# A two-layer decoder step in exact-split fp32: operand sums for the seven-product tiles moved to GpSimd, and the token mixes spread over the stage ahead and the first pair

## What is computed

```python
def swiglu(h, wg, wu, wd):
    return (jax.nn.silu(h @ wg) * (h @ wu)) @ wd
# D_MODEL = 1024, D_FF = 2816, all float32
x = x + 0.5 * swiglu(rmsnorm(x, norm), w_gate, w_up, w_down)
```

## Time and profile before

| | us |
|---|---|
| three runs: lowest, median, highest | 2516.43, 2526.86, 2526.91 |
| profiled execution, device time | 2519.78 |
| its span, first to last instruction | 2518.0 |
| around the span | 1.8 |

### The profile page before, as it was taken

One profiled execution on the slowest core, in us unless ns is written; L12 is line 12 of the kernel. 1 busy time (PEld: TensorE's weight loads), 2 busy tenths in 40 slices (PEclk: granted clock), 3 DMA queues, 4 the chain that ended last, 5 costly groups with the idle time before them and its releaser, 6 DMA issues. The chain is left out here.

```text
span 2518.0 us, 49302 instructions
## 1 busy us (share of the span) xinstructions
PE 2403.3 (95%) x18705; PEld 2335.5 (93%) x18705; DVE 1521.7 (60%) x2517; ACT 993.8 (39%) x1958; POOL 4.6 (0%) x18
## 2 busy tenths in 40 slices
PE   5999999998999999987999999999999999999998
PEld 5999999865999999977999999999999998999998
DVE  6864864555455555536863865873775656773772
ACT  5432433464455555524432434432433223432431
POOL 0000000000000000000000000000000000000000
PEclk8999999999999999989999999999999999999999
DMA  3323334310211111202333323233233332233232
GB/s 103 100 84 92 100 90 121 94 38 22 60 35 46 48 42 43 59 17 59 88 88 109 92 83 93 76 97 104 84 92 102 93 93 76 85 89 104 84 93 84
DMA packets 373200, 198.91 MB, mean 79 GB/s; under 512 B 31680, under 2 KB 369686, under 8 KB 373064
## 3 DMA queue, kind: packets, MB, share of 16 engines
q1 hardware_dynamic: 372884, 197.03, 27.3%
q10 hardware_dynamic: 180, 0.11, 0.0%
HBM read 194.27 MB, written 2.87 MB: 78 GB/s over the span
## 5 line engine op out<-in xcount | busy, mean ns | idle before, releaser
L408 PE MATMUL ps<-h_hi,w_hi 128*128 128x260 f32 x2112 | 435.9, 288 | 50.2 <-DVE w_lo L536 23.2
L397 DVE TENSOR_TENSOR w_lo<-raw,w_hi 128x512 fp32r<-128x512 f32 (+2 forms) x200 | 200.5, 1002 | 425.0 <-ACT w_hi L391 424.5
L410 PE MATMUL ps<-h_lo,w_hi 128*128 128x260 f32 x2112 | 431.4, 286 | 0.0
L412 PE MATMUL ps<-h_hi,w_lo 128*128 128x260 f32 x2112 | 431.0, 286 | 0.0
L408 PEld LDWEIGHTS ps<-h_hi,w_hi 128*128 128x128 f32 x2112 | 332.8, 193 | 53.7 <-DVE w_lo L536 24.1
L391 ACT CAST w_hi<-raw 128x512 fp32r<-128x512 f32 (+2 forms) x200 | 173.9, 869 | 510.8 <-PE ps L412 480.2
L412 PEld LDWEIGHTS ps<-h_hi,w_lo 128*128 128x128 f32 x2112 | 332.3, 192 | 0.0
L410 PEld LDWEIGHTS ps<-h_lo,w_hi 128*128 128x128 f32 x2112 | 332.1, 192 | 0.0
L408 PE MATMUL ps<-g_hi,w_hi 128*128 128x260 f32 x1408 | 285.1, 284 | 14.0 <-DVE w_lo L397 14.0
L531 ACT CAST w_hi<-raw 128x512 fp32r<-128x512 f32 x280 | 173.3, 622 | 286.5 <-PE ps L664 101.9
L412 PE MATMUL ps<-g_hi,w_lo 128*128 128x260 f32 x1408 | 283.9, 283 | 0.0
(11 more groups left out here) (351 smaller groups left out, 4208.9 us busy)
## 6 DMA issues: line engine op xcount, KB each, us to landing
raw<-in_w_ffn_gate SPq DMA_DIRECT2D x88, 512.0 KB, 3.9
raw<-in_w_ffn_up SPq DMA_DIRECT2D x88, 512.0 KB, 3.9
raw<-in_w_ffn_down SPq DMA_DIRECT2D x64, 448.0 KB, 3.7
raw<-in_w_ffn_down SPq DMA_DIRECT2D x64, 256.0 KB, 2.9
cache<-in_cache_latent SPq DMA_DIRECT2D x128, 128.0 KB, 2.0
raw<-in_w_conv_in SPq DMA_DIRECT2D x24, 512.0 KB, 3.7
raw<-in_w_o_attn SPq DMA_DIRECT2D x8, 512.0 KB, 4.0
cache<-in_cache_krope SPq DMA_DIRECT2D x128, 32.0 KB, 1.8
```

The lines of the kernel that those rows point to most:

```text
L397: nc.vector.tensor_tensor(w_lo[:, un.half, 0:n], src, w_hi[:, un.half, 0:n], ALU.subtract).then_inc(unit_lo_made, 1)
L408: nc.tensor.matmul(o[b], hi, mh[:, x0 + b * HALF:x0 + (b + 1) * HALF], start=start, stop=False)
L410: nc.tensor.matmul(o[b], hi, ml[:, x0 + b * HALF:x0 + (b + 1) * HALF], start=False, stop=False)
L412: mm = nc.tensor.matmul(o[b], lo, mh[:, x0 + b * HALF:x0 + (b + 1) * HALF], start=False, stop=stop)
```

## The change

**1.** The sums go to GpSimd as four 128x512 additions per pair in a loop of its own (`weight_sums`), with a counter `sums_made` that rises by 4 per pair; M5 and M7 wait for the second, M6 for the third, M3 for the fourth. `first_sums` and `more_sums` are gone from VectorE. **2.** Mixes are made one k at a time. Of ffn1 and ffn2 mixes 0 to 2, and of ffn3 mixes 0 and 1, are made in the stage ahead, when block k+4 of `xT` is ready (in mla's output stage between the block additions, elsewhere inside the publishing of block k+4). The remaining ones come after the first tile's hidden values; in ffn0 mix 0 comes there, and mixes 1 to 3 inside pair 0. **3.** Pair 0 of ffn0 has no seven-product tile: its second tile is plain (96 matmuls instead of 84), so 39 of the 40 pairs keep sums. **4.** The norm follows the split of CG0 and CG1 in all stages, and the split of CU comes right after the gate's silu or scaling. **5.** At a chunk's end VectorE splits `Unit(uc + 3)` between the additions L915 and L917, and TensorE waits for the last tile's `hid_done` only before the 11th tile of the first output block.

```diff
+        MIXED = {n: () if n == 0 else (0, 1) if stages[n - 1] == "conv" else (0, 1, 2)
+                 for n, s in enumerate(stages) if s[:3] == "ffn"}
...
-                act.wait_ge(sums_made, 3 * pr.n + {M5: 1, M7: 1, M6: 2, M3: 3}[q])
+                act.wait_ge(sums_made, SUMS * (pr.n - 1) + {M5: 2, M7: 2, M6: 3, M3: 4}[q])
...
+        def weight_sums(pool, pr):
             for j in (2, 3):
-                pr.loaded(dve, j)
+                pr.loaded(pool, j)
+            s = SUMS * (pr.n - 1)
+            g1, g2, u1, u2 = (pr.raw_half(2 + j // 2, j % 2) for j in range(4))
+            pool.wait_ge(part_lo_made, pr.step(M12 + 1))
+            nc.gpsimd.tensor_tensor(g1, g1, u1, ALU.add).then_inc(sums_made, 1)
+            pool.wait_ge(sums_made, s + 1)
+            nc.gpsimd.tensor_tensor(u1, u1, u2, ALU.add).then_inc(sums_made, 1)
+            pool.wait_ge(part_lo_made, pr.step(M4))
+            pool.wait_ge(sums_made, s + 2)
+            nc.gpsimd.tensor_tensor(u2, u2, g1, ALU.add).then_inc(sums_made, 1)
+            pool.wait_ge(sums_made, s + 3)
+            nc.gpsimd.tensor_tensor(g2, g2, u2, ALU.add).then_inc(sums_made, 1)
...
+        def mixes_dve(dve, n, ks, step):
             for k in ks:
+                dve.wait_ge(x_ready, KD * n + (KD if n == 0 else k + KH + 1))
                 mix_diff(dve, at, k)
-            for k in ks:
                 mix_sums(dve, n, at, k, step)
-            for k in ks:
                 mix_rest(dve, at, k)
+        def publish_mix_dve(dve, n, k, step):
+            mix_diff(dve, at, k - KH)
+            publish_dve(dve, n, k, middle=lambda: mix_sums(dve, n, at, k - KH, step))
+            mix_rest(dve, at, k - KH)
...
 ffn_dve:
-            if c == 0 and n:
-                mixes_dve(dve, n, at, (0, 1), step)
-                norm_dve(dve, n)
+            if c == 0 and n - 1 == CONV_NORM:
+                tails_dve(dve)
             part_lo(dve, nxt, CG0)
             part_lo(dve, nxt, CG1)
...
             scale_gate(0)
-            if c == 0:
-                mixes_dve(dve, n, at, (2, 3), step)
+            part_lo(dve, nxt, CU)
             dve.wait_ge(unit_used, uc + 2)
             scale_up(1)
             hid(t0)
-            part_lo(dve, nxt, CU)
+            if c == 0:
+                mixes_dve(dve, n, (0,) if n == 0 else [k for k in range(KH) if k not in MIXED[n]], step)
+            def plain_pair():
+                hid_rest(pr.t - 1, pr.f - 1)
+                scale_gate(2)
+                part_lo(dve, pr, M12)
+                scale_up(3)
+                hid(pr.t)
+                plain_up_lo(dve, pr)
+                hid_rest(pr.t, pr.f)
+                mixes_dve(dve, n, (1,), step)
+                part_lo(dve, nxt, CG0)
+                part_lo(dve, nxt, CG1)
+                scale_gate(0)
+                mixes_dve(dve, n, (2,), step)
+                part_lo(dve, nxt, CU)
+                scale_up(1)
+                hid(pr.t + 1)
+                mixes_dve(dve, n, (3,), step)
...
 ffn_dve, pair:
                 part_lo(dve, pr, M12)
-                first_sums(dve, pr)
                 part_lo(dve, pr, M5)
...
                 part_lo(dve, pr, M4)
-                more_sums(dve, pr)
                 part_lo(dve, pr, M6)
...
+                if last:
+                    split_lo(dve, Unit(uc + 3), DOWN[1] * P)
                 dve.wait_ge(added, add + 6)
...
 ffn_pe, down:
-                    if m == 0:
-                        pe.wait_ge(hid_done, t0 + CHUNK - 1 + p)
+                    if m == 0 and p == 0:
+                        pe.wait_ge(hid_done, t0 + CHUNK - 1)
...
+                        if m == 0 and k0 + k == CHUNK - 1:
+                            pe.wait_ge(hid_done, t0 + CHUNK)
```

More of the change, by code:

```diff
@@ L496, in __init__ @@
                 self.first = isinstance(it, int) and it == 0
+                self.plain = self.first and ch == 0
                 self.uc, self.it = chunk_u0[ch], it
@@ L567, in mix_diff, with mix_step @@
+        def mix_step(at, k):
+            return 3 * (KH * at + k)
         def mix_diff(dve, at, k):
@@ L714, in ffn_pe, with tile_half @@
                         pe.wait_ge(part_lo_made, pr.step(q if j == 0 else CU + 1))
[L715 to L720, removed]
+                        tile_half(2 + j, q, h).then_inc(part_used, 1)
+            def tile_half(s, q, h):
+                hi, lo = part(w_hi, q), part(w_lo, q)
+                for k in range(KH):
+                    kc = slice(k * P, (k + 1) * P)
+                    mm = product(s, hi[:, kc], lo[:, kc], h_hi, h_lo, KH * h + k, h == 0 and k == 0, h == 1 and k == KH - 1)
+                return mm
+            if ch == 0:
+                pr = Pair(ch, 0)
+                plain_tile(pr)
+                pe.wait_ge(part_lo_made, pr.step(M12 + 1))
+                pe.wait_ge(hid_done, pr.t)
+                tile_half(0, M12, 0).then_inc(part_used, 1)
+                tile_half(0, M12 + 1, 1).then_inc(part_used, M3 - M12)
+                pe.wait_ge(part_lo_made, pr.step(STEPS - 1))
+                tile_half(1, PLAIN_UP, 0)
+                tile_half(1, PLAIN_UP + 1, 1).then_inc(part_used, STEPS - 1 - M3)
+            with pe.Fori(int(ch == 0), PAIRS) as it:
+                pr = Pair(ch, it)
+                plain_tile(pr)
                 pe.wait_ge(part_lo_made, pr.step(M12 + 1))
@@ L811, in pair @@
                     part_hi(act, nxt, CU)
-            with act.Fori(0, PAIRS - 1) as it:
+            if ch == 0:
+                plain_pair()
+            with act.Fori(int(ch == 0), PAIRS - 1) as it:
                 pair(it, False)
@@ L968, in add_act @@
         def add_act(act, u0, n, publish=True):
[L970 to L974, removed]
+            for k in range(KD):
+                split_hi(act, Unit(u0 + k + 2))
+                mixed = k - KH in MIXED.get(n, ())
+                if publish and mixed:
+                    publish_mix_act(act, n, k)
+                elif publish:
+                    publish_act(act, n, k)
+                elif mixed:
+                    mixes_act(act, n, (k - KH,))
             if not publish:
@@ L977, in add_act, with add_dve @@
                     publish_act(act, n, k)
[L979 to L987, removed]
+        def add_dve(dve, u0, n, step, publish=True):
+            for k in range(KD):
+                split_lo(dve, Unit(u0 + k + 2))
+                dve.wait_ge(unit_used, u0 + k + 1)
+                xk = two(xT[:, k * T:(k + 1) * T])
+                nc.vector.tensor_tensor(xk, slot(k % 4), xk, ALU.add).then_inc(x_ready, 1)
+                mixed = k - KH in MIXED.get(n, ())
+                if publish and mixed:
+                    publish_mix_dve(dve, n, k, step)
+                elif publish:
+                    publish_dve(dve, n, k)
+                elif mixed:
+                    mixes_dve(dve, n, (k - KH,), step)
             if not publish:
@@ L2379, in _ @@
             start_pool(pool)
-            if "mla" in stages:
-                decode_pool(pool)
+            for s, u0 in plan:
+                if s[:3] == "ffn":
+                    for c in range(2):
+                        ch = 2 * FFN_AT[int(s[-1])] + c
+                        with pool.Fori(int(ch == 0), PAIRS) as it:
+                            weight_sums(pool, Pair(ch, it))
+                elif s == "mla":
+                    decode_pool(pool)
         @block.tensor
```

127 lines of the change are left out of this document (75 added, 52 removed).

## The result

The changed kernel took **2532.87 us** (median of 15 runs, 2531.28 to 2541.33); the kernel before, beside it, took 2526.55 us (15 runs, 2516.43 to 2529.85). The profiled execution took 2534.4 us, its span is 2532.6 us, 14.6 us more than the 2518.0 of the earlier trace rows.

What follows compares the result with a forecast made beforehand. TensorE was taken as the bound, busy 2403.3 of 2518.0 us. From 2519.8 us, chunk ends -14.0, steady pairs +16.1 and starts +1.1 gave 2523 us, forecast as no change, range 2503 to 2553.

Steps and rivals of the forecast that it cites:

- d: Length of one GpSimd addition of 512 columns in the sums, taken as 1.20 us from small memsets and affine selects.
- 4d - 4.34: Wait in us per steady pair before M6, with d the length of one GpSimd addition.
- the 35 pairs: Steady pairs, of 39 with sums: M6's split 0.46 us late in each, +16.1 us in all.
- The upper bound: Longest estimate for one GpSimd addition, with reads as dear as writes: 1.26 us.
- the deadline: In a steady pair, M6's split due at 2186.74 in the trace, expected at 2187.2, 0.46 us late.
- VectorE's split is held up while sum 4 runs: In each steady pair, M6's split was taken as delayed to the end of GpSimd's fourth addition, 0.46 us late.
- The sums are free: Rival: M6's split overlaps sum 4, no steady pair waits for d up to 1.26 us; 2504 us, chance 0.23.
- GpSimd is the new bound of each pair, slower: Rival: TensorE waits for sum 4 before M6; over 0.5% slower from d = 1.27 us, 2551 at 1.4; chance 0.27.
- A cold start: Rival: the first addition, in pair 1 of ffn0, pays the 11.24 us pause seen before; 2534 us, chance 0.08.
- Chunk ends: At eight chunk ends TensorE need not stop for the second down unit's split: 8 x 1.75 = 14.0 us won.
- Starts: Starts of ffn0 to ffn3: -1.1, +0.5, +0.2 and +5.5 us, less 4 for the clock: +1.1 us.
- The chain cost of 3.6 us: At each stage's start, TensorE waits at M5, M4 and M6 together for the chain of sums: 3.6 us.

Runs made afterwards that it cites:

- e5: The changed kernel with each of GpSimd's four additions cut to 128 of its 512 columns: 2493.32 us in one execution.
- e1: The changed kernel with the three sum instructions back on VectorE: 2493.4 us, ratio 0.987 to the kernel before.
- e2: The kernel before with the sums moved to GpSimd and nothing else changed: 2558.14 us, ratio 1.0124.
- e6: The changed kernel with only GpSimd's fourth addition cut, to 64 of 512 columns: 2507.71 us in one execution.
- e8: The changed kernel with the fourth sum replaced by an addition on 160 columns and a memset of the other 352: 2512.13 us in one execution.
- e3: The kernel before with only the chunk-end change (part 5): 2504.12 us, ratio 0.992.
- e1 again: The kernel of e1 measured once more, on the same chip as e10: 2490.41 us, ratio 0.987 to the kernel before.
- e10: The kernel of e1 with the mixes left at each stage's start moved behind M12's split: 2490.3 us, ratio 0.987 to the kernel before.

## Why the prediction was wrong

The measured time lies inside the stated range of 2503 to 2553; what came out otherwise is the direction. **The step that failed** is the duration of a GpSimd addition: "I take d = 1.20 us", drawn out from memsets and affine selects of at most 128 elements. It is 1.29. The prediction's own formula, 4d - 4.34, gives 0.82 us per pair with that, and 0.75 were measured; the 35 pairs cost 28.5 us instead of 16.1. Without these 12.4 us the changed kernel would have come out below the median of before; "each 0.1 us in d is 14 us" had warned of it. e5 shows that it is the length, e1 and e2 that it is the sums.

The upper bound was also worked out wrongly. With a read as dear as a write, give 0.10 us and 512 x 3 x 0.79 ns, which is 1.31 us and not 1.26. The measured 1.29 lies inside that bound, and the middle of 1.15 and 1.31 would have been d = 1.23. A smaller slip is in the deadline: 2181.84 + 2.1 is 2183.94, where 2183.86 stands. The rows of the kernel after side with the figure used, as L900 starts 0.08 us before the record of M5's split ends.

Within that step:

- *VectorE's split is held up while sum 4 runs*: right, and now shown by e6 and e8. It was put as ending 0.74 us after sum 4 and ended 0.54 after it (2220.07 to 2220.61), so the chain from M12's split to M6's took 9.47 us less four additions of 1.29, or 4.31, where the prediction had 4.55. Against that stood 0.05 us from the split to M6 and 0.11 for the restart, which the sum did not have. These nearly cancel, which is luck.
- *"The sums are free"*: fell, in both its conditions. The split does not overlap freely, and even without that d passes the 1.26 us up to which no pair would wait; e6 has the 0.22 us.
- *"GpSimd is the new bound of each pair, slower"*: this rival came true in kind: d passed its point of decision, 1.27. The 0.35% measured is below the 0.5% that it had named.
- *A cold start*: did not occur. The first addition, at 77.28 us, began as soon as M12 of its pair was split, and took 1.27 us. The same affine select that had begun 11.24 us late in the earlier trace rows began after 0.24 us here (first row of its kind on GpSimd's timeline):

```profile
1.43 0.29 POOL L2307 TENSOR_SCALAR_AFFINE_SELECT causal<-causal 128x128 f32<-128x128 f32 x1 [0.24 <-POOL causal L2306]
```

**Chunk ends**: right, 14.4 us for 14.0, and 15.9 in e1 and e3. The order on VectorE is as worked out; the last instruction before the split, the split itself, and its successor:

```profile
2270.64 0.43 DVE L995 TENSOR_TENSOR up_t<-ps,up_t 128x260 f32<-128x260 f32 x1
2271.80 1.09 DVE L399 TENSOR_TENSOR w_lo<-raw,w_hi 128x896 fp32r<-128x896 f32 x1 [0.74 <-ACT w_hi L393]
2272.81 0.42 DVE L999 TENSOR_TENSOR up_t<-up_t,ps 128x260 f32<-128x260 f32 x1
```

The 1.9 us more in e1 are 8 x 0.24: a stop costs a quarter of a microsecond more than its record says. In the kernel after 0.19 us of each are missing again; in ffn0's second chunk TensorE's first matmul of the down product starts 0.38 us behind the one ahead of it, where 0.12 is usual.

**Starts**: 4 us better than forecast, -2.9 for +1.1. The chain cost of 3.6 us at each was 4 x 3.6 = 14.4; e1 against the kernel after gives 11.0 (2.0, 4.2, 2.4 and 2.4). The rows show most of it as one wait of 1.6 to 2.0 us at M6 in each stage, with 0.19 at M5 in ffn1 alone and none at M4, where three waits had been put; where the rest lies was not followed. Of the waits, 3.94 us for CU in ffn0 was forecast as 3.8, 2.33 for M12 in ffn2 as 2.9, and 8.00 for M12 in ffn3 as 8.1. Without the chain the four stages were put at -4.7, -3.1, -3.4 and +1.9, and came in e1 to -3.9, -4.4, -4.8 and -0.8: 4.6 us better in all, against the 4 us that the sum gave the clock's recovery.

**The mla stage**: +3.4 us, where no instruction changed. It is scatter from execution to execution, and in these four it goes with the granted clock, the third number from the end in the windows over the stage (before, after, e1, e1 again):

```profile
410.95:1121.66 710.71, 675.75 (x4524) 615.26 (x4523) 378.13 (x834) 352.30 (x1005) 2.96 (x8) 0.98 0.17 49
```

```profile
411.62:1125.71 714.09, 678.21 (x4525) 616.78 (x4524) 378.01 (x835) 352.73 (x1005) 2.96 (x8) 0.97 0.18 49
```

```profile
403.08:1118.65 715.57, 679.46 (x4525) 616.82 (x4524) 377.97 (x835) 352.45 (x1005) 2.97 (x8) 0.97 0.18 49
```

```profile
401.10:1112.10 711.00, 675.55 (x4525) 615.47 (x4525) 377.94 (x834) 352.63 (x1005) 2.95 (x8) 0.98 0.18 49
```

The same matmuls keep TensorE busy for 2.5 to 3.9 us longer in the two executions with 0.97. Why the clock is lower in one execution than in another stays open.

**The base**: the sum was made against one execution of before with 2519.8 us, and the median of 15 is 2526.55. Against that the sum of +3.2 would have been 2529.8 us, some 3 below the result, and the measured difference of the medians, 6.3 us, is less than the 14.6 of the two spans. The executions of before go from 2516 to 2530 us, and the clock goes with them: of nine beside e10, the three above 2530 have a mean granted clock of 0.978 and the one of 2516.47 has 0.981. The prediction took 0.5% for what a measurement of this kernel can tell; 15 executions of each kernel told 0.35% apart, with 0.11% to either side.

What does it come to? The change has two parts of opposite sign. Chunk ends and mixes bring 1.3%, and e1, the kernel with those and the sums left on VectorE, beats both at 2493.4 and 2490.4 us. Moving the sums costs 1.2% in the kernel before (e2); in the kernel after it costs 1.6%, more than those gains.

## What to carry to other kernels

Moving work off an engine that the bound engine doesn't wait for wins nothing; what counts is the latency of the chain that it stands in, and here a slower engine's instruction entered it four times per pair, three times in the chain and once by lying over another engine's instruction. Price the largest uncertain duration so far that its error times its number stays below the answer you want to give: here 0.09 us decided the sign. When two engines are set side by side, look for the one whose record becomes longer, not only for idle time; and read a stop's cost from the start times around it, since the idle time in the row was 0.24 to 0.27 us short, and look at the granted clock behind it: in e2 a stop longer by 0.16 us cost 1.4 us more.

## What the runs showed of the hardware

- A GpSimd addition of two SBUF tiles took 1.29 us for 512 elements per partition, 0.53 for 160 and 0.32 for 64: 2.16 ns per element and some 0.18 us (0.46 for 128 in e5 fits). A copy of 352 took 0.48, a memset of 352 0.40. VectorE's split of 512, also with two inputs, takes 0.69. The small memsets and selects of the earlier trace rows had given 2.05 ns and 0.10 us, so 1.15 us: 0.08 is missing in the fixed part and 0.05 in the slope. The Trainium skill (GPSIMD Engine Reference, side-by-side cycle accounting) gives 4497 ns for 2048 elements; scaled in proportion that was 1.12 us, and the 1.3 us with a fixed part in it was the better reading. The line through these runs, drawn out to 2048 elements, is 4.6 us, within 3% of the page.
- A GpSimd instruction that reads SBUF holds up VectorE's subtraction of two SBUF tiles for all but 0.15 us of their overlap (overlaps of 0.26 to 0.69 us); a memset of GpSimd does not (0.17 to 0.26). GpSimd's own additions kept 1.29 us; here it was always GpSimd that had begun first.
- The pause of 11.24 us before GpSimd's first affine select is no property of the instruction alone: the execution of before has it, that of after does not, and nothing waited for it. Its cause is open.
- TensorE's granted clock fell to the lower level behind seven of e2's eight chunk-end stops of 1.91 us, and behind none of the eight of 1.75 us in the kernel before. One such stretch had 0.53, with 19 matmuls in 3.5 us where the kernel before has 31.
